# One block from the pool projection to w_out in a one-core pool/RWKV/ConvFFN decoder layer

## What is computed

```
h      = LN0(x) * (1 + scale1(c)) + shift1(c)          # mod = c @ ada_w, 6 x 1024 columns
proj   = h @ w_in    # columns r | k | v | 3 loras | pool | gate_pool | gate_rwkv
y      = rwkv7(r, decay, k, v, kk, a)                  # 16 heads of 64, group norm, bonus
y_rwkv = (y * g) @ w_branch_rwkv
mixed  = (moving averages of 2, 4, 8, 16 tokens - token) @ pool_w * pool_scale
y_pool = mixed @ w_branch_pool
merged = sigmoid(gate_pool) * y_pool + sigmoid(gate_rwkv) * y_rwkv
x      = LN1(ALPHA * x + (1 + gate1(c)) * (merged @ w_out))
x      = LN2(ALPHA * x + (1 + gate2(c)) * convffn(LN0(x) * (1 + scale2(c)) + shift2(c)))
```

## Time and profile before

| | |
|---|---|
| median of 3 runs | 1322.51 us (1320.77 to 1322.87) |
| profiled execution, its own time | 1320.41 us |
| its span in the trace | 1318.6 us |
| mean granted TensorE clock | 0.939 of 2.4 GHz |
| PE matmul busy | 1161.1 us, 88% |
| PE weight loads busy | 1047.9 us, 79% |
| DVE, ACT, POOL busy | 700.1, 490.4, 107.4 us |
| DMA queue q1 | 115.58 MB, 30.1% of 16 engines |

### The profile page before, as it was taken

The page is one execution under the profiler, slowest core; times in us unless marked ns, Lnnn a source line. Parts: engine busy times, 40 slices in busy tenths (PEclk is TensorE's granted clock), DMA queues, the critical chain, the costliest instruction groups (busy, mean ns, idle before and its releaser), DMA issues.

```text
span 1318.6 us, 35055 instructions
## 1 busy us (share of the span) xinstructions
PE 1161.1 (88%) x15404; PEld 1047.9 (79%) x15404; DVE 700.1 (53%) x1118; ACT 490.4 (37%) x799; POOL 107.4 (8%) x153
## 2 busy tenths in 40 slices
PE   4868999999999985868699999969999999969995
PEld 1357888888888863845599999969899899969995
DVE  2144666666666653493333343676666667643226
ACT  0434444534534523233322222355443443432221
POOL 0001220220220220200000000130000000000000
PEclk9979999999999997865799999989999999979998
DMA  8331022022021001589432336232233232252221
GB/s 269 112 101 48 8 56 56 4 55 56 3 56 40 4 4 38 173 210 302 119 100 80 95 87 197 77 104 74 66 93 94 65 95 81 59 172 82 80 79 65
DMA packets 185471, 117.36 MB, mean 89 GB/s; under 512 B 6684, under 2 KB 177490, under 8 KB 185065
## 3 DMA queue, kind: packets, MB, share of 16 engines
q1 hardware_dynamic: 185353, 115.58, 30.1%
HBM read 108.40 MB, written 7.34 MB: 88 GB/s over the span
## 4 chain that ended last, share of the span: by engine, by line
PE 27%; issue 9%; DVE 8%; ACT 7%; POOL 1%; DVEq 1%; ACTq 0%; POOLq 0%
PE PJ L225 21%; PE PJ L217 4%; ACT Wh L1706 2%; ACT ACC L1847 2%; DVE ACC L2118 2%; DVE ACC L2119 1%; DVE ACC L2126 1%; DVE ACC L2124 1%; ACT ACC L1845 1%; DVE Wl L1897 1%; PE BB L225 0%; ACT SFh L1854 0%; PE BB L217 0%; DVE M L1907 0%; PE BB L1657 0%
## 5 line engine op out<-in xcount | busy, mean ns | idle before, releaser
L225 PE MATMUL PJ<-Hh,Wh 128*128 128x260 f32 (+2 forms) x1056 | 237.4, 307 | 44.1 <-DVE Wl L1897 23.3
L1897 DVE TENSOR_TENSOR Wl<-RAW,Wh 128x1024 fp32r<-128x1024 f32 (+1 forms) x104 | 120.8, 1164 | 196.9 <-ACT Wh L1706 191.3
L225 PEld LDWEIGHTS PJ<-Hh,Wh 128*128 128x128 f32 x1056 | 167.5, 193 | 63.6 <-issue 31.2
L225 PE MATMUL PJ<-Hh,Wl 128*128 128x260 f32 (+2 forms) x1056 | 216.8, 287 | 1.3 <-issue 1.3
L225 PE MATMUL PJ<-Hl,Wh 128*128 128x260 f32 (+2 forms) x1056 | 217.4, 288 | 0.0
L225 PEld LDWEIGHTS PJ<-Hh,Wl 128*128 128x128 f32 x1056 | 167.5, 192 | 1.5 <-issue 1.5
L225 PEld LDWEIGHTS PJ<-Hl,Wh 128*128 128x128 f32 x1056 | 167.5, 193 | 0.0
L1706 ACT ACTIVATE Wh<-RAW 128x1024 fp32r<-128x1024 f32 (+1 forms) x108 | 108.6, 1010 | 104.8 <-PE PJ L225 103.2
L2118 DVE SCALAR_TENSOR_TENSOR ACC<-ACC,CP 128x512 f32<-128x512 f32 x88 | 66.0, 750 | 71.5 <-ACT ACC L1847 69.8
L1166 POOL TENSOR_TENSOR MO<-BP,CST 128x512 f32<-128x512 f32 x40 | 55.7, 1401 | 308.8 <-DVE KP L1049 251.7
L225 PE MATMUL PJ<-SFh,Wh 128*128 128x256 f32 (+1 forms) x308 | 64.5, 291 | 13.4 <-DVE Wl L1897 13.4
(11 more groups left out here) (369 smaller groups left out, 2317.8 us busy)
## 6 DMA issues: line engine op xcount, KB each, us to landing
RAW<-in_w_in_dram SPq DMA_DIRECT2D x46, 512.0 KB, 4.2
RAW<-in_ffn_up_dram SPq DMA_DIRECT2D x44, 512.0 KB, 3.8
RAW<-in_ada_w_dram SPq DMA_DIRECT2D x32, 512.0 KB, 6.1
RAW<-in_ffn_down_dram SPq DMA_DIRECT2D x16, 512.0 KB, 3.9
RAW<-in_ada_w_dram SPq DMA_DIRECT2D x2, 2048.0 KB, 10.7
ACC<-in_ada_w_dram SPq DMA_DIRECT2D x2, 2048.0 KB, 13.3
RAW<-in_w_branch_rwkv_dram SPq DMA_DIRECT2D x8, 512.0 KB, 3.9
RAW<-in_w_out_dram SPq DMA_DIRECT2D x8, 512.0 KB, 4.0
```

The lines of the kernel that those rows point to most:

```text
L225: mm = pe.matmul(out[:, b, 0:nb[b]], w[:, slot, kw, :], x[:, kx, c0:c0 + nb[b]], start=first and w is Wh and x is xh, stop=last and w is Wl)
L1897: dve.tensor_tensor(Wl[:, slot, 0:kn], RAW[:, slot, 0:kn], Wh[:, slot, 0:kn].bitcast(F32), ALU.subtract).then_inc(S("w_lo"), 1)
```

## The change

The two blocks become one, and its products stand in another order: 4 pool projections, all 16 gate projections (`B_GATE`), 8 pool branches (`B_PB`), 8 rwkv branches (`B_RB`), 8 w_out. The gates are kept as `GP`, `GR`. Behind gate p on PE (p = 1 to 16, the last behind the first pool branch) stands `ada_batch(p)`: the turns of the modulation tiles 2(p-2), 2(p-2)+1 and the rows of 2(p-1), 2(p-1)+1. The modulation tiles have three slots of their own (`RAW` slot 3 and slot 3 of `Wh`, `Wl`) in place of four; the weights have a ring of three. The recurrence is cut into halves of 128 x 2048, between the DVE's weight splits. The square root stands in ACT's work after gate 10. The 25 small loads of constants become 4, and `pool_w` and the state are loaded ahead of the fourth pool weight. The output of the new state stands in SP's loop at p = 10. The YG split goes into `Hh`, `Hl` and under the pool branches. The loop over e is unrolled; the row loads for LN1 come earlier.

The core of the diff:

```diff
-                for n in range(NA):
-                    if n == 0:
-                        sp.wait_ge(S("w_lo"), B_POOL + NPOOL)
-                    if n > 3:
-                        sp.wait_ge(S("ada_used"), n + 1)
-                    sp.dma_start(RAW[:, n % 4], cols("ada", 2 * KT + n)).then_inc(S(f"ld_ada{n % 4}"), 16)
...
+                def load_ada(n):
+                    if n >= 3:
+                        sp.wait_ge(S("ada_used"), n + 2)
+                    sp.dma_start(AD[n % 3], cols("ada", 2 * KT + n)).then_inc(S(f"ld_ada{n % 3}"), 16)
...
+                for p in range(1, NG):
+                    load(B_GATE + 2 + p)
+                    for n in (2 * p + 1, 2 * p + 2):
+                        if n < NA:
+                            load_ada(n)
...
+                    if p == 10:
+                        sp.wait_ge(S("s_new"), 1)
+                        sp.dma_start(o["wkv_s"][0].rearrange("b h v k -> (b h) (v k)"), S0[:].rearrange("p v k -> p (v k)")).then_inc(S("out"), 16)
...
             @block.tensor
+                def ada_batch(p):
+
+                    if p == 2:
+                        pe.wait_ge(S("po"), 1)
+                    if p >= 2:
+                        for n in range(2):
+                            ada_turn(2 * (p - 2) + n)
+                    if p <= NA // 2:
+                        if p == 1:
+                            pe.wait_ge(S("mf"), NPOOL)
+                        for n in range(2):
+                            ada_rows(2 * (p - 1) + n)
...
+                for p in range(NG):
+                    n = B_GATE + p
+                    pe.wait_ge(S("w_lo"), n + 1)
+                    if p < 2:
+                        pe.wait_ge(S("pn"), p + 3)
+                    else:
+                        pe.wait_ge(S("sg_p"), p - 1)
+                    for k in range(KT):
+                        mm = kstep(pe, PJ[p % 2], slot_of(n), k, Hh, Hl, k, k == 0, k == KT - 1, nb)
+                    mm.then_inc(S("prj"), 1)
...
+                    else:
+                        ada_batch(p)
...
             @block.scalar
+                for p in range(NG):
+                    act.wait_ge(S("prj"), B_GATE + p + 1)
...
+                    gate = GP[:, p, :] if p < KT else GR[:, p - KT, :]
+                    act.activation(two(gate), PJ[p % 2][:, :, 0:260], ACT.Sigmoid).then_inc(S("sg_p"), 1)
+                    split_n(B_GATE + 3 + p)
...
+                    else:
+                        ada_batch(p)
```

More of the change, by code:

```diff
@@ L1500, in _ @@
+                sp.wait_ge(S("mgl"), 2)
+                sp.dma_start(XAS[:], i["x_sample"][:, 0, :]).then_inc(S("ld_x"), 16)
+                for n in range(B_OUT, B_FF):
+                    if n == B_OUT + 3:
+                        sp.wait_ge(S("ada_used"), NA + 4)
+                    load(n)
                 for q in range(4):
@@ L1529, in _, with mix @@
                     sp.dma_start(o["y_p"][0, t * P:(t + 1) * P, :] if t < 4 else o["y_s"][:, 0, :], x_row2(t)).then_inc(S("st"), 16)
+                sp.wait_ge(S("out"), 16 * 5)
+                sp.wait_ge(S("po_out"), 32)
                 sp.wait_ge(S("st"), 16 * (5 + 14 + 5))
+            def mix(pe, g):
+                past(pe, "ld_cst", 16)
+                pe.wait_ge(S("df"), g + 1)
+                after(pe, "mf", g)
+                for b in range(2):
+                    mm = pe.matmul(B[2 + b][:, 0:260], PW[:, g, :], DF[:, 260 * b:260 * b + 260], start=True, stop=True)
+                mm.then_inc(S("mm_mix"), 1)
@@ L1548, in _ @@
-                tile(0)
-                with pe.Fori(1, KT) as e:
-                    tile(e)
+                for c in range(KT):
+                    b, r = divmod(c, 4)
+                    mm = pe.transpose(B[b][0:6 * NS, r * P:(r + 1) * P], SMP[:, c].rearrange("p q b -> p (q b)"), ident)
+                mm.then_inc(S("t_vt"), 1)
+                for q in range(NPOOL):
+                    n = B_POOL + q
+                    pe.wait_ge(S("w_lo"), n + 1)
+                    after(pe, "pn", q - 1)
+                    for k in range(KT):
+                        mm = kstep(pe, PJ[q % 2], slot_of(n), k, Hh, Hl, k, k == 0, k == KT - 1)
+                    mm.then_inc(S("prj"), 1)
+                    if q > 0:
+                        mix(pe, q - 1)
@@ new lines, in ada_rows @@
+                def ada_rows(n):
+                    pe.wait_ge(S(f"ld_ada{n % 3}"), 16 * (n // 3 + 1) + (32 if n % 3 < 2 else 0))
+                    pe.wait_ge(S("mod_rows"), n + 3)
+                    for k in range(KT):
+                        g = k % 4
+                        mm = pe.matmul(B[2 + n % 2][32 * g:32 * g + 32, 0:P], CT[:, k, :], AD[n % 3][:, k, :], start=k < 4, stop=k >= 4,
+                                       tile_position=(0, 32 * g))
+                    mm.then_inc(S("ada_used"), 1)
@@ new lines, in _ @@
+                for e in range(KT):
+                    split_n(B_PB + 3 + e)
+                    if e < 2:
+                        ada_batch(NG + e)
+                    if e >= 2:
+                        if e == 2:
+                            act.wait_ge(S("ygs"), 1)
+                        if e < 6:
+                            for c in range(2 * (e - 2), 2 * (e - 2) + 2):
+                                act.activation(YGh[:, c, :], YG[:, c, :], ACT.Copy).then_inc(S("ygh"), 1)
+                act.wait_ge(S("out"), 16 * 5)
@@ L1731, in split_out @@
+                for e in range(KT):
+                    split_n(B_RB + 3 + e)
+                    act.wait_ge(S("mg"), e + 1)
+                    act.activation(MGh[:, e, :], GR[:, e, :], ACT.Copy).then_inc(S("mgh"), 1)
                 def split_out(e):
-                    split(B_OUT + e, e % 4, br_loads[e % 4] + 16 * KT + 16 * (e // 4), ring=4)
+                    split_n(B_OUT + e)
                 def split_ff(q):
```

663 lines of the change are left out of this document (332 added, 331 removed).

## The result

The change is slower, by 0.6%. Its median is 1330.5 us (17 runs, 1323.1 to 1336.3) against 1322.7 us for the kernel before (17 runs, 1319.3 to 1326.3): ratio 1.0057, 95% interval 1.0042 to 1.0071, or 7.9 us more where 9.5 less was forecast against the median (7.3 by its sum). The profiled execution took 1331.6 us; the span is 1329.8, the mean granted clock 0.938, PE is busy 1168.8 us (88%).

A forecast was written before the change was run, and what follows sets the result against it. Branch loop bound by PE, modulation by its loads; overlapped, a four-engine loop sets the pace. X(1) 570.6 + 149.8 − 2.6 + 5 + tail 77 = 799.8 against 807.1, so 1320.4 − 7.3 = 1313 us; range 1300 to 1330.

The forecast's parts named there:

- The loop through SP, the DMA, ACT and PE: Gates: a batch's rows release three loads, then ACT's split and copies, then PE's next turns; this sets the pace.
- I take 10.7 us per gate: Gate loop: each round takes 10.7 us against 7.6 of PE work; fourteen rounds, 149.8 us.
- turn 0.32, rows 0.58: Gate loop, PE's part of a round: one turn 0.32 us and its rows 0.58, together 0.9.
- X(3): End of the first modulation rows of batch 3; X(p) is that moment for batch p, forecast X(1) 570.6, X(15) 722.8.
- the 5 us for the state's output: Gate loop at p = 10: the 2 MB output ahead of a weight load adds 4.8, say 5 us.
- 0.7 us, from 0 to 4: Pool stage: GpSimd's outer product holds up DVE, so the averages of group 1 reach PE 0.7 us late.
- the tail: From X(15) through pool and rwkv branches to the last rwkv product: 77 us, 0.5 of it for x rows.
- what is hidden: Under gates and pool branches: the recurrence, square root with table loads and YG split cost nothing.
- The break-even case: Gate rounds of 11 to 11.4 us, break-even 11.2, from dearer hand-overs: no change, 1318 to 1323 us; chance 0.12.
- the slow one: Gates: PE's idle time lowers its clock, rounds of 13.9 us; in every second round 22 us more, 1335; chance 0.18.
- the forecast: Gate rounds of 10.1 to 11 us, kernel 1304 to 1318 us; chance 0.62.
- the rival of PE's pace: Gates: loads do not queue, rounds 7.6 to 8.5 us, 1267 or 1282; sign: DMA share far from full; chance 0.08.

The follow-up runs named there:

- e1: The change with SP issuing the weight load ahead of the two modulation loads (one more weight loaded ahead of the loop): 1272.9 us, ratio 0.962 to the kernel before.
- e2: The change with ACT making biases and copies ahead of the weight split, SP's order unchanged: 1277.7 us, ratio 0.968 to the kernel before.
- e5: The change with the weight load between the two modulation loads (one more weight loaded ahead of the loop): 1299.7 us, ratio 0.984 to the kernel before.
- e9: The change profiled again with no edit, one execution: 1330.1 us.
- e11: The change with 24 extra unused matmuls of 260 columns on PE ahead of each batch's turns: 1325.8 us, ratio 1.0034 to the kernel before.
- e3: The change with GpSimd's outer product waiting until gate 1 is done: 1323.7 us, ratio 1.0017 to the kernel before.
- e7: The change with the 2 MB of x rows for LN1 loaded behind the sixth rwkv weight, not the second: 1325.3 us, ratio 1.0021 to the kernel before.
- e8: The change with the edits of e1, e2, e3, e6 and e7 together: 1260.7 us, ratio 0.953 to the kernel before.
- e6: The change with the 2 MB state output moved from p = 10 to behind the last pool weight: 1320.4 us, ratio 0.9994 to the kernel before.

## Why the prediction was wrong

- **The mechanism held.** The loop through SP, the DMA, ACT and PE was predicted, with its releasers (ACT's split by the DMA, the turns by the copies `UO`), and e1, e2, e5 each move it. PE busy 80% in the rounds, against the 72% predicted, is in part the low clock, at which the same work takes longer.
- **Failed: "I take 10.7 us per gate".** The break-even was put at 11.2, and the rounds without the last two and p = 10 average 11.3 in the change (11 rounds, 124.7 us). By the parts of the sum, the mean of these 11 rounds:

| part of a round, us | predicted | change | e9 |
|---|---|---|---|
| end of the first rows to SP's issue | 0.2 | 0.05 | 0.05 |
| issue to the split (three loads) | 7.7 | 8.16 | 8.25 |
| split to the turns (split, biases, copies, hand-over) | 1.96 | 1.57 | 1.57 |
| turns and first rows | 0.9 | 1.55 | 1.50 |
| sum | 10.76 | 11.33 | 11.37 |

  The step that failed most is PE's part, "turn 0.32, rows 0.58". It has one turn, but a batch begins with two, and it has the full clock. From the start of the turns to the end of the first rows it took 1.20 us at the full clock and 2.03 at the low one (a batch of e9 at the low clock, then one of e11 at the full, on PE):

```profile
644.89 1.02 PE L1404 MATMUL BB<-CST,UO 128*128 128x9 f32 x4 [2.39 <-ACT UO L1661]
645.84 1.08 PE L1397 MATMUL BB<-RAW,CT 128*32 128x128 f32 x16
646.70 1.08 PE L1397 MATMUL BB<-AD,CT 128*32 128x128 f32 x16
```
```profile
641.02 0.61 PE L1404 MATMUL BB<-CST,UO 128*128 128x9 f32 x4 [0.18 <-ACT UO L1665]
...
641.57 0.65 PE L1397 MATMUL BB<-RAW,CT 128*32 128x128 f32 x16
```

  The loads come second, 0.46 us dearer on the mean: they took 7.6 to 8.2 us, but for one round of 10.3 (without it the mean is 7.95). The two small outputs ahead of the weight at p = 3 (1.25 + 0.29, which the sum left out) did not lengthen theirs: the split began 7.82 us behind X(3). Together the rounds took 160.3 against 152.2: 7.0 more in these eleven, 1.0 at p = 10 and 0.1 in the last two.
- **Right: the 5 us for the state's output.** From the issue to the split it was 13.0 us where 7.7 + 5 was said. The round took 16.7 and not 15.7, for the most part because PE's part stood at the low clock; without the output it takes 10.2.
- **Failed: "0.7 us, from 0 to 4" for the outer product.** The start of GpSimd's instruction was right: 541.1 is 538.6 on the scale of before (its block starts 2.6 earlier), and 538 was said. What it meets was wrong. The sum held up only the averages of group 1, which PE wants about 6 us later; the instruction fell into those of group 0, which PE wants at once. The stage took 5.9 more (e3 gives 5.6 back): a wait of 3.94 and the low clock behind it, for the most part. Whatever small operation such an instruction may meet, a term's upper end has to be its whole length.
- **Nearly right: the tail.** 84.7 against 83.2. The 2 MB of x rows cost PE 2.19 us and the low clock behind it, 3 to 4 us by e7 and not 0.5; the rest of the tail was 1 to 2 us shorter than its sum.
- **Right: what is hidden.** The recurrence, the square root and the YG split cost nothing that shows, and in e8 they lie under a PE that never waits. w_out starts at once.
- **The rivals.** The break-even case and the slow one had 0.30 between them. The result, 1330.5, lies just beyond the upper end of the range of 1300 to 1330, but by another way than the rival on the slow side: the clock was granted low behind most waits and full again later in the gate, 0.84 in the mean, and that comes to some 5 us of the 160 (e11), not 22. What made the kernel slower was a sum of small terms: each of the three stages took longer than said, by 5.9, 8.1 and 1.5. The sign that was named for the rival of PE's pace, a DMA share far from full, was there (0.52) although the rounds took 11.3, so it was no sign of that rival. With a break-even only 0.5 us per round away, a chance of 0.62 for the forecast was too much.
- **Missed altogether:** that the loop could be broken by moving one load in a queue. The rival with PE's pace (rounds of 7.6) describes e1 and e8, which came to rounds of 7.3.

Open: why single loads land late (p = 5 in the change and in e6, p = 2 in e9); and what e6 gained beyond the 6.5 us of its round.

## What to carry to other kernels

Here the work that was moved under other work paid only once its releases and those of the other work no longer made a chain through the same queues (e1, e2). Write down, for one iteration, what each in-order queue (SP's loads above all) holds *ahead* of a load and who releases it; a load that isn't wanted for two iterations, behind loads that are released in this one, and an engine that stands at it, make a loop whose latency is the pace, and one load moved ahead of two others (e1) or one swap on ACT (e2) was worth more here than the whole move. Where the gain per round is half a microsecond and there are fourteen rounds, count every instruction on the loop, and measure stages from the last unchanged event before them.

## What the runs showed of the hardware

- A DVE multiplication of 128x16 with two inputs in SBUF took 7.05 us beside a GpSimd multiplication of 128x4096, in place of 0.18; one of 128x512 (e9) took 7.43 in place of 0.69. Both started within 0.25 us of the large one's start and ended with it; a copy of 128x8, with one input, that started 0.01 us behind the large one in e9 took its usual 0.16.
- In the rounds of the change PE waited 0.9 to 7.1 us before each batch. Behind those of 1.4 us and more the granted clock fell to 1.2 GHz (pairs 0.43 to 0.44 us apart) and was back at 2.4 GHz (0.24 apart) 4 to 7 us behind the end of the wait; behind those of 0.93, 1.14 and 1.34 us it stayed at 2.4. In e9 three gates ran at 2.4 GHz throughout although waits of 1.94, 2.48 and 2.83 us stood before their batches, so not each such wait has that effect. With matmuls in the wait the clock stayed up (0.98 in e11 against 0.84). The Trainium skill (TensorE: Matmul & The Clock Gate, HAM oscillation) says that groups of matmuls with a DMA wait between them start cold each time; most rounds agree, these few do not, and the loss was some 5 us of 160, since most of a gate lay off the path.
- One 512 KB load less ahead of a weight was worth 2.3 us in each round, 2.0 of it transfer (e5), and the 2 MB ahead of it 6.5 us in the one round (5.7 of it up to the split), while the mean DMA share was only 0.52: a share far from full says nothing about the latency of the load that is waited for.
